# A two-block transformer kernel on one core: modulation sums, transposes and context statistics moved one step earlier, and root spreads rebuilt from diagonals

## What is computed

```python
def rmsnorm(x, g):
    return x * lax.rsqrt(jnp.mean(x * x, axis=-1, keepdims=True) + RMS_EPS) * g

# block 1
mod = silu(c) @ mod_w + mod_b            # sh_m, sc_m, gt_m, sh_f, sc_f, gt_f
h = rmsnorm(x, norm_pre_mix) * (1.0 + sc_m) + sh_m
y = conformer_conv_module(h, ...)        # pw1, GLU, 31 taps, layernorm, silu, pw2
x = x + gt_m * rmsnorm(y, norm_post_mix)
h = rmsnorm(x, norm_pre_ffn) * (1.0 + sc_f) + sh_f
u = causal_dwconv(h @ w_up, dw_w) + dw_b # 3 taps
gt, v = split(u)
x = x + gt_f * rmsnorm((silu(gt) * v) @ w_down, norm_post_ffn)

# block 2: the same frame with its own modulation ("ada"); ctx has 256 tokens
hc = modulate(rmsnorm_2(ctx, g_mix_pre), csh1, csc1)
proj = modulate(rmsnorm_2(x, g_mix_pre), sh1, sc1) @ w_in
y_hy = hyena_branch(proj[..., :OFF_Q]) @ w_hy_up     # short conv, long conv by FFT
o = diff_attention(q, k_all, v_all, lam)             # 4 heads, keys of x and of ctx
y_att = (rmsnorm_2(o, subln_g) * (1.0 - lam_init)) @ w_att_up
mixed = (g_hy * y_hy + g_att * y_att) @ w_out
x = x + g1 * rmsnorm_2(mixed, g_mix_post)
f = swiglu(modulate(rmsnorm_2(x, g_ffn_pre), sh2, sc2), ...)
x = x + g2 * rmsnorm_2(f, g_ffn_post)
```

## Time and profile before

| | |
|---|---|
| time, median of 3 runs | 3354.58 us (3352.52 to 3355.29) |
| the profiled execution | 3355.29 us, its span 3353.5 us |
| busy | PE 3125.0 us (93%), DVE 1637.9 (49%), ACT 1010.8 (30%), POOL 426.5 (13%) |
| mean granted clock of TensorE | 0.953 |
| DMA | 301.24 MB, mean 90 GB/s |

### The profile page before, as it was taken

The page is one execution under the profiler, slowest core; times in us unless marked ns, Lnnn a source line. Parts: engine busy times, 40 slices in busy tenths (PEclk is TensorE's granted clock), DMA queues, the critical chain, the costliest instruction groups (busy, mean ns, idle before and its releaser), DMA issues.

```text
span 3353.5 us, 33558 instructions
## 1 busy us (share of the span) xinstructions
PE 3125.0 (93%) x13822; PEld 2514.2 (75%) x13822; DVE 1637.9 (49%) x1752; ACT 1010.8 (30%) x1203; POOL 426.5 (13%) x177
## 2 busy tenths in 40 slices
PE   6898878999999999989999998889988999999996
PEld 2683557778888888778888876777767788888885
DVE  3777665566556564574521055577435422222225
ACT  2344445242222221233321123467222221111111
POOL 0396760000000000000200033100010000000000
PEclk8998887899999999989999999999998999999998
DMA  5113442223223222221332243442321112111112
GB/s 203 44 45 106 142 147 79 72 87 102 77 74 126 96 94 81 101 76 63 123 121 102 94 151 132 110 99 53 110 95 71 68 48 63 41 44 63 32 51 107
DMA packets 96193, 301.24 MB, mean 90 GB/s; under 512 B 11206, under 2 KB 15046, under 8 KB 95848
## 3 DMA queue, kind: packets, MB, share of 16 engines
q1 hardware_dynamic: 96040, 299.09, 27.3%
HBM read 251.34 MB, written 47.71 MB: 89 GB/s over the span
## 4 chain that ended last, share of the span: by engine, by line
PE 81%; DVE 9%; ACT 3%; issue 3%; DMA 2%; POOL 1%; SPq 0%; DVEq 0%; ACTq 0%; POOLq 0%
PE ps L705 67%; PE ps L751 3%; PE ps L766 2%; PE ps L1093 2%; PE ps L1118 2%; PE ps L808 1%; DVE ps L1990 1%; PE ps L1103 1%; DVE tmp L1864 1%; PE ps L793 1%; DVE mainf L1857 1%; DMA mainr<-sc_k 1%; DVE tmp L2264 1%; DVE mainr L1871 1%; DVE tmp L2258 1%
## 5 line engine op out<-in xcount | busy, mean ns | idle before, releaser
L705 PE MATMUL ps<-mainr,wh 128*128 128x512 f32 (+1 forms) x7104 | 1943.4, 391 | 42.5 <-POOL wl L2415 11.5
L705 PEld LDWEIGHTS ps<-mainr,wh 128*128 128x128 f32 x7104 | 1335.6, 189 | 322.5 <-issue 46.0
L705 PE MATMUL ps<-mainr,wl 128*128 128x512 f32 (+1 forms) x3552 | 1130.9, 389 | 0.0
L705 PEld LDWEIGHTS ps<-mainr,wl 128*128 128x128 f32 x3552 | 671.7, 189 | 139.1
L1214 ACT CAST wh<-raw 128x1024 fp32r<-128x1024 f32 (+2 forms) x320 | 281.8, 886 | 726.5 <-PE ps L705 549.5
L1688 DVE TENSOR_TENSOR wl<-raw,wh 128x1024 fp32r<-128x1024 f32 (+2 forms) x256 | 248.0, 970 | 465.5 <-ACT wh L1214 465.4
L2415 POOL TENSOR_TENSOR wl<-raw,wh 128x1024 fp32r<-128x1024 f32 x64 | 154.4, 2419 | 454.5 <-ACT wh L1214 454.5
L751 PE MATMUL ps<-mainr,wh 128*128 128x512 f32 x576 | 167.2, 414 | 40.8 <-issue 27.4
L1947 DVE TENSOR_TENSOR mainf<-mainf,ps 128x1024 f32<-128x1024 f32 x80 | 97.6, 1220 | 215.1 <-PE ps L705 215.1
L1990 DVE SCALAR_TENSOR_TENSOR ps<-mainf,vec,ps 128x1024 f32<-128x1024 f32 (+1 forms) x174 | 180.9, 1102 | 0.8 <-ACT ps L1403 0.7
L2453 POOL TENSOR_TENSOR tmp<-tmp,mainf 128x1024 f32<-128x1024 f32 x8 | 27.5, 3442 | 1179.2 <-DMA mainf<-in_rope 1117.3
(11 more groups left out here) (228 smaller groups left out, 2583.9 us busy)
## 6 DMA issues: line engine op xcount, KB each, us to landing
raw<-in_mod_w SPq DMA_DIRECT2D x48, 512.0 KB, 4.5
raw<-in_ada_w SPq DMA_DIRECT2D x48, 512.0 KB, 3.6
raw<-in_f_up SPq DMA_DIRECT2D x44, 512.0 KB, 4.2
raw<-in_g_up SPq DMA_DIRECT2D x44, 512.0 KB, 3.5
raw<-in_w_in SPq DMA_DIRECT2D x40, 512.0 KB, 4.1
raw<-in_pw SPq DMA_DIRECT2D x24, 512.0 KB, 3.6
sc_x<-mainf SPq DMA_DIRECT2D x24, 512.0 KB, 2.6
mainf<-sc_x SPq DMA_DIRECT2D x24, 512.0 KB, 6.1
```

Of the source, the lines that this page charges most:

```text
L705: ins = e.matmul(out, wt[:, a:b], xs[n], start=kk == 0 and t == 0, stop=kk == kt - 1 and t == 2)
```

## The change

The change has five parts.

1. `SUMMED` begins at (1, 0) instead of (2, 0): every pair of modulation pieces stands one FFN half step earlier among the weights, the first behind f_up(1, 0).
2. `turned` runs one tile behind the convolution instead of two, on all three engines. On ScalarE the reversed copy of tile f now stands ahead of it.
3. The context statistics, their sum and their normalisation move from f = 9, 10, 11 to 8, 9, 10.
4. `scale` becomes `diagonal`: behind the reciprocal VectorE multiplies the identity by each of the eight columns and by 1024 (eight products of 128x128, into one slot of the ring `tmp`). `spread` is then two fp32 matmuls of 512 columns with `ones` as the stationary operand and these diagonals as the moving one, each behind its four products. `head_spread` is one such matmul. In `block_end` the second reciprocal, with its products, moves behind `scaled(0)`.
5. In the second FFN, GpSimd adds squares 1 to 6 into `k.S(0)` (`squares_added`), and the columns of this sum move from the inside of the last tile to behind it.

```diff
-    out, at = {}, (2, 0)
+    out, at = {}, (1, 0)
...
@@ TensorE
-    def spread(s, out, roots):
-
-        w.wait_ge(*k.at("rec", s))
-        w.wait_ge(*k.at("ident", 0))
-        for c in range(8):
-            ins = e.matmul(out[:, 128 * c:128 * c + 128], roots[:, c:c + 1].broadcast_to([128, 128]), m.ident[:, :],
-                           start=True, stop=True)
+    def spread(s, out, *key):
+        t = k.TMP(*key)
+        for n in range(2):
+            w.wait_ge(*k.at("dg", s, 4 * n + 3))
+            ins = e.matmul(out[:, 512 * n:512 * n + 512], m.ones[:, :], t[:, 512 * n:512 * n + 512], start=True, stop=True)
         ins.then_inc(*k.to("spread", s))
...
     def square_columns(s):
+        w.wait_ge(*k.at("yacc", s, ND - 2))
+        columns(k.S(0), True, False, "y" + s, 0)
         w.wait_ge(*k.at("ysq", s, ND - 1))
         columns(k.TMP("ysq", s, ND - 1), False, True, "y" + s, 1)
...
-                squares = c == LAST and (i if s == "f" else i == ND - 1)
+                squares = s == "f" and c == LAST and i
...
-        if 2 <= f <= 9:
-            turned(f - 2)
-        if f == 10:
+        if 1 <= f <= 8:
+            turned(f - 1)
+        if f == 9:
             hold_aux("ctx", banks=(0,))
             w.wait_ge(*k.at("cxadd", 1, 3))
...
     def head_spread(hd, half):
         hold_pt("spread", hd, half)
-        w.wait_ge(*k.at("rec", "o", hd))
-        for c in range(4):
-            r = k.COL("rs", 4 * half + c)
-            ins = e.matmul(k.PT[:, 128 * c:128 * c + 128], r.broadcast_to([128, 128]), m.ident[:, :], start=True, stop=True)
-        ins.then_inc(*k.to("ospread", hd, half))
+        w.wait_ge(*k.at("odg", hd, 4 * half + 3))
+        e.matmul(k.PT, m.ones[:, :], k.TMP("diag", "o", hd)[:, 512 * half:512 * half + 512], start=True,
+                 stop=True).then_inc(*k.to("ospread", hd, half))
...
@@ ScalarE
-        if 2 <= f <= 9:
-            turned(f - 2)
         if f < 8:
             w.wait_ge(*k.at("hy2", f))
             hold_tmp("rev", f)
             e.copy(k.TMP("rev", f)[:, 0:512], t[:, T - 1:511:-1]).then_inc(*k.to("rev", f))
-        if f == 9:
+        if 1 <= f <= 8:
+            turned(f - 1)
+        if f == 8:
             for i in range(2):
...
@@ VectorE
-    def scale(s, rs="rs"):
+    def diagonal(s, *key, rs="rs"):
 
         rs = k.COL(rs, 0, 8)
         w.wait_ge(*k.at("sqrt", *s))
         e.reciprocal(rs, rs).then_inc(*k.to("rec", *s))
+        w.wait_ge(*k.at("rec", *s))
+        hold_tmp(*key)
+        t = k.TMP(*key)
+        for c in range(8):
+            ins = e.tensor_scalar(t[:, 128 * c:128 * c + 128], m.ident[:, :], rs[:, c:c + 1], 1024.0, ALU.mult, ALU.mult)
+            ins.then_inc(*(k.to("odg", s[1], c) if s[0] == "o" else k.to("dg", s[0], c)))
...
         split_to(k.W[keys[2]] + 1)
-        scale(("y" + s,))
+        diagonal(("y" + s,), "diag", "y" + s)
         mean_square(s)
-        scale((n,), "rn")
...
         scaled(0)
+        diagonal((n,), "diag", n, rs="rn")
         summed(0)
         normed(0)
...
-                if s == "g" and c == LAST and 0 < i < ND - 1:
-                    w.wait_ge(*k.at("ysq", s, i))
-                    w.wait_ge(*k.at(*(("yacc", s, i - 1) if i > 1 else ("ysq", s, 0))))
-                    e.tensor_tensor(k.S(0), k.S(0), k.TMP("ysq", s, i), ALU.add).then_inc(*k.to("yacc", s, i))
...
@@ GpSimd
+    def squares_added(s):
+        for i in range(1, ND - 1):
+            w.wait_ge(*k.at("ysq", s, i))
+            if i > 1:
+                w.wait_ge(*k.at("yacc", s, i - 1))
+            e.tensor_tensor(k.S(0), k.S(0), k.TMP("ysq", s, i), ALU.add).then_inc(*k.to("yacc", s, i))
...
+    squares_added("g")
     for i in (1, 3, 5):
```

More of the change, by code:

```diff
@@ L467, in residual_plan @@
             self.acc.take(("res", s), ("rmul", s, ND - 1))
+            self.tmp.take(("diag", "y" + s), ("spread", "y" + s))
             return
@@ L485, in norm_plan @@
     def norm_plan(self, s):
+        self.tmp.take(("diag", s), ("spread", s))
         self.aux_take(("spread", s), [("premul", s, ND - 1)], [("premul", s, ND - 1)])
@@ L586, in plan @@
         self.aux[0].take(("cols", "ln"), ("sqrt", "ln"))
+        tmp.take(("diag", "ln"), ("spread", "ln"))
         self.aux_take(("spread", "ln"), [("lnmul", ND - 1)], [("lnmul", ND - 1)])
@@ L798, in norm_spread @@
         hold_aux("spread", s)
-        spread(s, aux, k.COL("rn" if s in ("n2", "n3", "n4") else "rs", 0, 8))
+        spread(s, aux, "diag", s)
     def normed(s, hi, lo):
@@ L840, in residual @@
         hold_acc("res", s)
-        spread("y" + s, k.ACC("res", s), k.COL("rs", 0, 8))
+        spread("y" + s, k.ACC("res", s), "diag", "y" + s)
     def block_end(s, x, ready):
@@ L983, in tensor_program @@
     sum_columns("ln")
-    norm_spread("ln")
+    hold_aux("spread", "ln")
+    spread("ln", aux, "diag", "ln")
     project("pw2", pairs(lambda kk: 8 + kk, lambda kk: 16 + kk), lambda kk: [("lnhi", kk), ("lnlo", kk)])
@@ L2087, in vector_program @@
     w.wait_ge(*k.at("ident", 0))
-    scale(("n1",))
+    diagonal(("n1",), "diag", "n1")
     split_to(k.W["pw1", 0] + 3)
@@ L2138, in vector_program @@
     split_to(k.W["pw2", 0] + 3)
-    scale(("ln",))
+    diagonal(("ln",), "diag", "ln")
     w.wait_ge(*k.at("spread", "ln"))
@@ L2351, in vector_program @@
             if qt == 6:
-                scale(("o", hd - 1))
+                diagonal(("o", hd - 1), "diag", "o", hd - 1)
             if qt == 7:
@@ L2374, in vector_program @@
     head_sums(NH - 1)
-    scale(("o", NH - 1))
+    diagonal(("o", NH - 1), "diag", "o", NH - 1)
     hyena_gate(0)
```

19 lines of the change are left out of this document (8 added, 11 removed).

## The result

The changed kernel takes 3380.44 us (median of 4 runs, 3379.19 to 3384.65) against 3354.48 for the kernel before on the same chip: +26.0 us where +25.4 was forecast. The record has 17 more executions of the changed kernel; all 21 run from 3379.19 to 3388.97, with a median of 3383.44. The ratio on record, 1.0087 (95% interval 1.0075 to 1.0098), is that of all 21: +29 us (25 to 33). So the four timings lie at the low end, and the loss is 26 to 29 us. The profiled execution took 3385.08 us (span 3383.3), 1.6 above the median of all.

A forecast was written before the change was run, and what follows sets the result against it. TensorE's matmuls were taken to set the pace, so only its stops counted. The terms summed to +25.4 on the profiled 3355.29, giving 3380.7, and 3380 as median (0.7 lower); range 3366 to 3391.

The forecast's parts named there:

- Modulation sums: First FFN: weight f_up(1,1) falls behind FFN step 0, its tile starts 7.7 us later, 2.0 lost to clock; +9.7 us.
- Transposes: w_in: tile 3 starts 5.4 us later behind 16 transposes, less low clock saved; +4.8 us.
- Context: Context statistics in w_in: TensorE waits before the context sum for additions behind the context load; +2.0 us.
- Diagonals: Spreads through diagonals: layernorm +0.9 us; block ends' norm spreads +3.3 at n2 and n4, +1.8 at n3, together +8.4.
- Attention: Attention: eight products ahead of a maximum for three heads, mostly covered by key-load waits and VectorE's gaps; +0.5 us.
- tail: Second FFN's end: square-sum columns move into TensorE's wait for the last square, -1.8, diagonal +0.9; -0.9 us.
- Rival A: New spreads and the work after new stops run at full clock; sum +12.2 us, 3367; chance 0.16.
- B: Diagonal products cost 0.40 us each at exposed places and in attention; about +13 more, 3393; chance 0.15.
- C: Spreads: the wide 512-column fp32 pass is fast, nine spreads save 25 to 30 us; 3350 to 3355; chance 0.06.

The follow-up runs named there:

- e3_turn: The kernel before with only the transposes of w_in moved one tile earlier, context statistics in their old place; measured +4.1 us, ratio 1.0015.
- e2_diag: The kernel before with only the diagonal spreads (spread, head_spread, diagonal and block_end edits); measured +8.2 us, ratio 1.0029.

## Why the prediction was right

The forecast of 3380 lies at the timed 3380.44, and 3 below the median of all 21 executions (3383.44). By its own steps, against the trace:

1. *Modulation sums*, +9.7: measured 11.9 in the changed kernel's trace and 10.6 alone, by trace and by time. The 7.7 later start and the 2.0 of clock are there as worked out. What is above them in the trace is another 2.1 us of slower matmuls elsewhere in that FFN; no step of the forecast has them, and up to 1.5 of them is what kernels without the change scatter by.
2. *Transposes*, +4.8: 3.5 by the trace alone, 4.1 by time. The later start (5.35 against 5.4) was right. The half clock, of which I left 1.6, took about 0.6 in the changed kernel and 1.3 in e3_turn.
3. *Context*, +2.0: the wait is 2.15 in the changed kernel, and for the additions as forecast. Alone it is 1.83, with ScalarE's copy as the one that ends it, and +3.4 by time with a wide interval.
4. *Diagonals.* The cost of a product, which no row showed, was 0.20 from start to start as taken. The layernorm's +0.9 and the block ends' +3.3 held at n2 (3.0). At n3 the price of 1.8 assumed the full clock of the old trace and the spread had half: 3.4. At n4 I took half and it was partly full: 2.5. Together 8.9 for a forecast 8.4. The Trainium skill (VectorE: DVE Perf Modes, the errata table) gave 0.13 us a product, with the remark in the same section that this row of its table gives too little; the trace does not agree with 0.13, and 0.20 decides.
5. *Attention* and *tail*: -0.3 for +0.5, and -0.9 as forecast. In the attention the products did cost waits (2.1 us more of standing still), and 2.3 us less of busy time at a better clock took them back; that was not forecast, and the small term came out by luck.

The errors (+2.2, -1.3, +0.5, -0.8) partly cancel; that the total comes within 1 us of the four timings is luck, that the stops and their lengths are those of the forecast is not.

Rival A is out: the stops are followed by half clock and the spreads are slow at n2. (Its sum also has only one term for attention and context, 0.5 named context, where the forecast has 0.5 and 2.0.) Its page, the Trainium skill (TensorE: Matmul & The Clock Gate, What's actually happening), would have the spreads at full clock after so long an activity. The traces agree in part: n3's 32 records took 5.56 and the second of e2_diag 2.37, but n2's took 6.60, with the clock at 0.50. B is out by 0.20 against 0.40 a product. C is out: a spread by two wide matmuls took 3.75 at half clock, as eight narrow ones did, and in the attention at full clock one wide took 1.12 and four narrow ones 1.16.

## What to carry to other kernels

Where every engine runs one list in order, moving cheap work earlier moves what stands behind it later. Look for the first item that now has to cross a stage boundary: of 26 to 29 us, 11 came from one weight that fell behind FFN step 0, and 9 from eight small products that stood behind a scaling that itself waited. Both were free a few positions further ahead.
